# Three fused blocks on one core: low-rank inputs of the middle block inside its projection, and four junctions computed by halves of the tokens

## What is computed

```python
def second_block(x, ...):
    h = rmsnorm(x, pre_mix_g)
    proj = h @ w_in                                  # "win2"
    ya, yb, yc = split(proj)
    a_out = rwkv7_mixer(ya, ...)                     # token shift, low-rank decay, chunked recurrence
    b_out = moba_mixer(*split(yb, 3))                # attention
    c_out = gmlp_mixer(*split(yc, 2), ...)
    mix = concat(a_out, b_out, c_out) @ w_out        # "wout2"
    x = x + rmsnorm(mix, post_mix_g)
    h = rmsnorm(x, pre_ffn_g)
    gate, up = split(h @ w_ffn_in)                   # "ffin2"
    f = (silu(gate) * up) @ w_ffn_out                # "ffout2"
    return x + rmsnorm(f, post_ffn_g)

def rwkv7_mixer(ya, ...):
    prev = pad(ya)[:, :-1]
    ya = ya + mu * (prev - ya)                       # token shift
    r, k, v, wd, ad, gd = split(ya)
    w = -softplus(-(w0 + tanh(wd) @ w2)) - 0.5       # low-rank decay input
    a = sigmoid(a0 + ad @ a2)                        # low-rank input
    g = sigmoid(gd) @ g2
    kk = normalised(k * k_k)
    ...

def third_block(x, ...):
    h = rms_norm(x, norm_mix_pre)                    # then "win3a"
    x = x + rms_norm(hybrid_mixer(h, ...), norm_mix_post)      # ends in "wout3"
    f = square(relu(rms_norm(x, norm_mlp_pre) @ w_ff1)) @ w_ff2   # "ff1_3", "ff2_3"
    return x + rms_norm(f, norm_mlp_post)
```

## Time and profile before

| | |
|---|---|
| median of 3 runs | 3485.95 us |
| profiled execution | 3472.73 us, its span 3470.8 us |
| TensorE busy | 3293.9 us (95% of the span) |
| VectorE, ScalarE busy | 1159.3 us (33%), 553.4 us (16%) |
| chain that ended last | TensorE 84%, DMA 8%, VectorE 4%, ScalarE 3%, issue 1% |
| mean granted TensorE clock | 0.972 of full speed |

### The profile page before, as it was taken

How to read it: one execution, slowest core, us unless ns; L and a number is a source line. 1 busy time by engine, 2 the same in 40 slices (tenths; PEclk the granted TensorE clock), 3 DMA queues, 4 the chain that set the end, 5 groups by cost and what they waited for, 6 DMA issues and landing times.

```text
span 3470.8 us, 33312 instructions
## 1 busy us (share of the span) xinstructions
PE 3293.9 (95%) x13642; PEld 1788.8 (52%) x13642; DVE 1159.3 (33%) x2215; ACT 553.4 (16%) x1100; POOL 1.4 (0%) x6
## 2 busy tenths in 40 slices
PE   7999899999999999998799899999999999999998
PEld 4555444344333333376785378844444444378543
DVE  2046531111111111155653254401351893254101
ACT  2033220110011001213122310001232002200000
POOL 0000000000000000000000000000000000000000
PEclk9999999999999999999888999999999999999999
DMA  5122338999999999910000121212111221112210
GB/s 236 49 73 98 112 155 355 428 429 428 428 428 429 429 429 428 383 73 35 1 1 6 71 94 73 97 73 75 73 49 50 90 78 73 73 73 93 77 73 24
DMA packets 41082, 585.13 MB, mean 169 GB/s; under 512 B 4688, under 2 KB 4688, under 8 KB 5392
## 3 DMA queue, kind: packets, MB, share of 16 engines
q1 hardware_dynamic: 40752, 582.45, 41.2%
q0 software_dynamic: 224, 1.18, 0.1%
HBM read 581.51 MB, written 2.10 MB: 168 GB/s over the span
## 4 chain that ended last, share of the span: by engine, by line
PE 84%; DMA 8%; DVE 4%; ACT 3%; issue 1%; SPq 0%; DVEq 0%; ACTq 0%
PE PS L243 27%; PE PS L339 15%; PE PS L1139 10%; DMA ring<-in_weights 8%; PE PS L1119 4%; PE PS L547 3%; PE PS L279 3%; PE PS L730 3%; PE PS L1073 2%; PE PS L1936 2%; PE PS L1106 1%; PE PS L687 1%; PE PS L1055 1%; PE PS L553 1%; PE PS L1597 1%; PE PS L1924 1%
## 5 line engine op out<-in xcount | busy, mean ns | idle before, releaser
L243 PE MATMUL PS<-A,ring 128*128 128x512 f32 x1608 | 703.7, 600 | 15.1 <-DVEq L2215 7.2
L243 PEld LDWEIGHTS PS<-A,ring 128*128 128x128 f32 x1608 | 307.9, 192 | 407.3 <-issue 388.2
L1139 PE MATMUL PS<-A 128*64 128x512 f32 x1280 | 294.0, 601 | 2.3 <-DMA A<-in_weights 1.1
L339 PE MATMUL PS<-A 128*128 128x256 f32 x1056 | 235.1, 379 | 0.0
L243 PE MATMUL PS<-H,ring 128*128 128x512 f32 x544 | 234.3, 592 | 0.0
L339 PEld LDWEIGHTS PS<-A 128*128 128x128 f32 x1056 | 200.6, 190 | 27.3
L1119 PE MATMUL PS<-ring,A 128*64 128x512 f32 x768 | 173.2, 597 | 17.6 <-DMA ring<-in_weights 17.4
L1211 DVE TENSOR_TENSOR A<-A,PS 64x512 f32<-64x512 f32 x64 | 44.2, 690 | 420.9 <-ACT A L1168 420.9
L1139 PEld LDWEIGHTS PS<-A 128*64 128x64 f32 x1280 | 85.1, 137 | 176.9 <-issue 168.7
L1139 PE MATMUL PS<-ring,A 128*64 128x512 f32 x768 | 175.4, 598 | 0.8 <-DMA ring<-in_weights 0.3
L1514 DVE COPY H<-PS 128x512 f32<-128x512 f32 x32 | 22.1, 692 | 456.1 <-ACT A L1533 456.1
(11 more groups left out here) (448 smaller groups left out, 3511.7 us busy)
## 6 DMA issues: line engine op xcount, KB each, us to landing
ring<-in_weights SPq DMA_DIRECT2D x178, 2048.0 KB, 14.1
A<-in_weights SPq DMA_DIRECT2D x96, 2048.0 KB, 24.0
X<-in_x SPq DMA_DIRECT2D x1, 2048.0 KB, 10.8
out_y<-X SPq DMA_DIRECT2D x4, 512.0 KB, 2.6
con<-in_const SPq DMA_DIRECT2D x1, 1423.0 KB, 6.4
vec<-in_vec SPq DMA_DIRECT2D x1, 1075.0 KB, 15.0
A<-in_ctx SPq DMA_DIRECT2D x1, 1024.0 KB, 12.8
con<-in_levels POOLq DMA_DIRECT2D x1, 896.0 KB, 4.9
```

Of the source, the lines that this page charges most:

```text
L243: mm = nc.tensor.matmul(bank[:, 0:out_width], weight_tile(name, n), moving(k), start=k == 0, stop=k == k_tiles - 1)
L339: mm = nc.tensor.matmul(pair_bank(p, n), w[:, k, :], x[:, k, :], start=k == 0 and not more, stop=k == 3, skip_group_check=more)
L1139: mm = nc.tensor.matmul(PS[CAP * up:CAP * (up + 1), c % 2, :], XS[:, k, CAP * b:CAP * (b + 1)], w[:, n:n + 4, :].rearrange("p a b -> p (a ...
```

## The change

In the second block the token shifts begin with LO, GD and the keys, in pairs 4 to 9; `block1_out` runs twice a pair in pairs 0 to 3; k times k_k stands in pair 6. ScalarE takes tanh of LO and sigmoid of GD in pair 5. TensorE runs the six low-rank products in pair 6, after its second quarter product, in the four banks that the pair doesn't use, and ScalarE drains them there with sigmoids. After win2 VectorE does the running sums for p = 0 first, then the floors, p = 1, the normed MG, p = 2, two preparations, the gMLP gate, the third preparation. Tiles move in the arena so that nothing overlaps; the gate's banks are 6 and 7.

At the junctions the last output tile is computed for tokens 0 to 255 and then for 256 to 511, in two banks; ScalarE squares and copies each half, and mean, Ln, Exp, scaling, sum and `raw` are done by halves. The first half's mean stands on TensorE's queue after k = 3 of the second half, the second half's mean after k = 1 of the next projection's first half. `first_products` runs its four tiles over the first half and then over the second; the mean for the next norm comes after k = 2 of the second half. The number after `raw` is how many of the first half's tiles ScalarE makes before it turns to the second half's Ln and Exp (4, 8 and 4). At the end the output leaves in 2 transfers for the first half and 4 for the second.

```diff
+        def first_products_by_halves(pe, name, raw, sq):
+            base = S.next("pe", "raw", 16) - 16
+            banks = [open_bank(name, f) for f in range(4)]
+            for h in range(2):
+                for k in range(8):
+                    pe.wait_ge(S["raw"], base + 8 * h + k + 1)
+                    for f in range(4):
+                        mm = nc.tensor.matmul(banks[f][:, half_of(h)], weight_tile(name, 8 * f + k),
+                                              raw(k)[:, half_of(h)], start=k == 0, stop=k == 7)
...
+                    if h == 0 and k == 1:
+                        half_mean(pe, 1, sq)
+                    if h == 1 and k == 2:
+                        pe.wait_ge(S["sumsq"], S.next("pe", "sumsq"))
+                        nc.tensor.matmul(PS[:, 5, :], mean, H[:, 0, :], start=True, stop=True).then_inc(S["mean"], 1)
+        def half_mean(pe, h, sq):
+            if h == 0:
+                pe.wait_ge(S["msum"], S.next("pe", "msum"))
+            nc.tensor.matmul(PS[:, 5 + h, half_of(h)], mean, sq(0)[:, half_of(h)], start=True, stop=False)
+            pe.wait_ge(S["msq"], S.next("pe", "msq", 1 if h else 8))
+            nc.tensor.matmul(PS[:, 5 + h, half_of(h)], mean, sq(7)[:, half_of(h)], start=False, stop=True
+                             ).then_inc(S["mean"], 1)
+        def products_by_halves(pe, name, k_tiles, moving, sq):
+            products(name, range(7), k_tiles, moving)
+            for h in range(2):
+                for k in range(k_tiles):
+                    n = 7 * k_tiles + k
+                    mm = nc.tensor.matmul(PS[:, 4 + 3 * h, half_of(h)], weight_tile(name, n), moving(k)[:, half_of(h)],
+                                          start=k == 0, stop=k == k_tiles - 1)
...
+                    if h and k == 3:
+                        half_mean(pe, 0, sq)
+                mm.then_inc(S["last"], 1)
...
+        def last_half_act(act, h, sq):
+            act.wait_ge(S["last"], S.next("act", "last"))
+            bank = PS[:, 4 + 3 * h, half_of(h)]
+            nc.scalar.activation(sq(7)[:, half_of(h)], bank, ACT.Square).then_inc(S["msq"], 1)
+            nc.scalar.activation(H[:, 7, half_of(h)], bank, ACT.Copy)
...
+            if split < 8:
+                last_half_act(act, 1, sq)
+            pre_norm_half(act, 0, range(split), gain, raw)
+            nc.scalar.preload_act_table(ACT.Ln)
+            if split == 8:
+                last_half_act(act, 1, sq)
+            half_power_act(act, 1)
+            pre_norm_half(act, 0, range(split, 8), gain, raw)
+            pre_norm_half(act, 1, range(8), gain, raw)
             power_act(act)
...
-            post_norm_act(act, "wout2", RAW)
-            pre_norm_act(act, "pre_ffn", RAW)
+            post_norm_act(act, "wout2", RAW, "pre_ffn", RAW, 4)
...
             for p in range(10):
                 fast_out_dve(dve, "win2", p, a(4 + 2 * p), a(5 + 2 * p))
-                if p < 8:
-                    block1_out_dve(dve, p)
-                for j in (2 * p - 8, 2 * p - 7):
-                    if 0 <= j < 11:
-                        token_shift_dve(dve, j)
+                if p < 4:
+                    block1_out_dve(dve, 2 * p)
+                    block1_out_dve(dve, 2 * p + 1)
+                else:
+                    for n in (2 * p - 8, 2 * p - 7):
+                        if n < 11:
+                            token_shift_dve(dve, n)
...
-            for j in range(4):
-                sp.wait_ge(S["x_new"], 32 + 2 * j + 2)
-                sp.dma_start(out[:, 2 * j:2 * j + 2, :], X[:, 2 * j:2 * j + 2, :]).then_inc(S["stored"], 16)
+            for h, tiles in ((0, 4), (1, 2)):
+                for k in range(0, 8, tiles):
+                    sp.wait_ge(S["x_new"], 56 + 8 * h + k + tiles)
+                    sp.dma_start(out[:, k:k + tiles, TC * h:TC * h + TC], X[:, k:k + tiles, TC * h:TC * h + TC]
+                                 ).then_inc(S["stored"], 16)
```

More of the change, by code:

```diff
@@ L54 @@
     ("gate2", 0, 0, 3),
-    ("wout2", 8, 8, 8),
+    ("wout2", 8, 8, 7),
     ("ffin2", 2 * NFF2, 8, 4),
-    ("ffout2", 8, NFF2, 8),
+    ("ffout2", 8, NFF2, 7),
     ("win3a", 8, 8, 8),
@@ L343, in product @@
                     mm.then_inc(S["quarter"], 1)
+                if name == "win2" and p == LORA_PAIR + 1:
+                    all_drained(pe, "lora2", 6)
                 product(0, A11, HQ[0][0])
@@ L349, in fast_products @@
                 product(1, S2, T2)
+                if between:
+                    between(p)
                 if p == 0:
@@ L1851, in rwkv_tensor @@
         def rwkv_tensor(pe):
-            pe.wait_ge(S["lora_in"], 2)
-            for f in range(6):
-                bank = open_bank("lora2", f)
-                rows = slice(0, 64) if f < 3 else slice(64, 128)
-                nc.tensor.matmul(bank, vec[rows, VOFF["w2a2"][0] + f % 3 * P:VOFF["w2a2"][0] + (f % 3 + 1) * P],
-                                 A[rows, LO, :], start=True, stop=True).then_inc(S["product"], 1)
             for j in range(2):
```

195 lines of the change are left out of this document (116 added, 79 removed).

## The result

| | before | after |
|---|---|---|
| median (range, runs) | 3487.72 us (3485.44 to 3490.47, 4) | 3440.24 us (3439.24 to 3441.34, 4) |
| ratio after / before | | 0.9878 (95%: 0.9853 to 0.9902) |
| profiled execution | 3472.73, span 3470.8, clock 0.972 | 3439.27, span 3437.5, clock 0.978 |

The change is faster by 47.5 us by the medians, and by 33.5 by the two profiled executions. The forecast was 3461, with 3473 and 3453 as its ends: right in sign, wrong in size, and the median lies outside that range.

A forecast was written before the change was run, and what follows sets the result against it. TensorE, busy 95% of the span, bounds the kernel; only idle or slow stretches can be won. 8.2 + 4.1 + 3.3 + 8.1 + 4.5 = 28.2 us, less 3.4 for the clock, 24.8: 3485.95 - 24.8 = 3461 us, range 3453 to 3473.

The forecast's parts named there:

- the last one of the sum: Whole program: 24.8 us gained, taken off the runs' median 3485.95 rather than the profiled execution's 3472.73, giving 3461 us.
- Rival D: Recurrence behind the changed chain: short bursts hold the lower clock, 45 us longer, ending 20 us slower, 3506; chance 0.03.
- The second block: Win2's last quarter product to last preparation: 41.2 us for 54.6, 13.4 earlier; less 5.15 in pair 6, 8.2 gained.
- The low-rank term: Win2's pair 6: six low-rank calls, 12 records x 0.429 = 5.15 us longer, a cost.
- rival B: Second block gives nothing: TensorE waits in pairs 5 to 7 or the chain keeps its length; 16.6 gained, 3469; chance 0.12.
- ffout2's 8.1: Junction after ffout2: no gap left, 128 records and two means end at 2447.8 and not 2455.91, 8.1 us gained.
- wout2's 4.1: Junction after wout2: TensorE idle 2.7 us for 5.89, 4.1 us gained, before 1.7 us lost to the clock.
- rival A: Junctions after wout2 and wout3: the clock does not fall behind 2.7 us gaps; 28.2 us gained, 3458; chance 0.24.
- wout3's: Junction after wout3: same code as wout2's, 3.3 us gained, before 1.7 us lost to the clock behind a 2.7 us gap.
- Rival E: Junctions: halves run one behind the other, only the end and second block gain; 12.7 us, 3473; chance 0.06.
- Rival C: Junctions with 4 tiles ahead: a ScalarE table switch holds 1.38 us longer, TensorE starts 1.4 us later, 3464; chance 0.05.
- The end: Program's end: chain about 0.3 us shorter, 16 half-width VectorE instructions 6.0 us for 10.2, store stays 3.0; 4.5 us gained.

The follow-up runs named there:

- e1: The kernel before, unchanged, run again: median 3478.68 us, 6 executions short and 6 long.
- e4: The changed kernel, unchanged, run again: median 3441.29 us, 6 executions short and none long.
- e16: The changed kernel run again on another comparison's chip: median 3440.06 us, ratio to before 0.9889.
- e3: The changed kernel with its second block's part taken back, so only junctions and end go by halves: median 3464.17 us.
- e6: The kernel before with two useless calls on 64 rows in TensorE's idle time ahead of the last preparation's transposes: median 3473.09 us, 5 of 12 long.
- e7: The changed kernel with useless 128-row calls in TensorE's idle times at the junctions and ahead of wout2, ffout2, wout3 and ff2_3: median 3436.47 us.
- e9: The changed kernel with the MLP gate's four VectorE instructions back ahead of the three preparations: median 3460.64 us, 6 of 7 long.
- e10: The kernel before with only the gate's four VectorE instructions moved between the second and third preparation: median 3484.98 us, 9 of 12 long.
- e13: The changed kernel with the gate's four VectorE instructions moved on behind the start of the inverse: median 3454.05 us, 6 of 6 long.

## Why the prediction was wrong, point by point

**The step that failed** is the last one of the sum: "That execution is 13.2 us below the median of the runs, so for the median it is 3485.95 - 24.8". It took the 13.2 us as something that any kernel would carry along. They came from one stretch of before, the products within chunks, which by their lengths ran at the lower clock in 74 of 107 executions and then took 33.6 us for 17.5 (e1's profile and before's); none of the 16 executions of the change is long. Of the 20.9 us between 3461.15 (3485.95 - 24.8) and 3440.24, 13.2 are this offset, 8.7 is what the two profiled executions differ by beyond the 24.8 (4.3 at the attention's end, 2.6 before win2, the rest small), and 1.0 goes off again, because the change's profiled execution lies that far below its own median. So even against the profiled execution alone the 24.8 us were a quarter short of the 33.5 measured.

**Rival D had the mechanism and the wrong sign.** It said that the short bursts meet the clock at another time now, put the loss at 45 us, and ruled it out because "the runs of before, which meet it by chance too, lie within 5 us". The numbers at hand said otherwise: three runs at 3485 to 3490 and a profile at 3472.7 were two lengths, not a spread of 5. The stretch that differs is also another than the one D named (from 1800 us on): it lies at 1675 to 1708 us. The prediction's own last sign of being wrong, that "the stretch from the chunks within to wout2 has another length than before", holds against the long executions of before (16 us) and not between the two profiles (from the last transposes to wout2's start 253.1 us for 253.3).

**The second block.** From win2's last product to the last preparation 41.3 us for a forecast 41.2, the normed MG at +14.8 for +14.6: each step of that chain held within 0.3 us. The low-rank term was mis-sized: 3.81 us for 5.15, because records of 64 rows took 0.32 us where the sum had 0.429. The cover was there: no engine is late in pairs 5 to 7, so rival B falls. The earlier trace rows had a hint in them: 6.76 us for twelve records is little for records of 0.43 to 0.86, and before's clock stood at 0.50 for the first 6.0 of them.

**The junctions.** ffout2's 8.1 us held, and wout2's 4.1 measured 4.0, because the clock did not fall behind its 2.62 us gap (forecast 2.7), as rival A had it. Behind wout3's it did, and a second time behind the 3.04 us wait (forecast 3.2) further on: 3.4 us there, nothing at wout2, for 1.7 at each. The sum of the two was right, by luck. Rival E falls: the halves overlap. Rival C falls too, TensorE began when the forecast said.

**The end**: 5.0 us for 4.5; from the first scaling to the last sum 5.9 us for a forecast 6.0, the chain began 0.4 us earlier for 0.3, and the store behind the last sum, which the sum left at 3.0, took 2.7.

**Not foreseen**: 4.3 us at the attention's end, and 2.6 us before win2. The latter differ from one execution to the next and are no gain of the change: e4's trace of the same program is later by 2.7 us at win2's end and at its own end, e16's by 0.9 and 0.8.

## What to carry to other kernels

Where a profiled execution lies apart from the timed ones by more than these spread, ask first which stretch makes the difference, and profile the kernel again until both lengths are at hand; a constant offset is a guess that can be as large as the gain. Here the stretch was a long run of matmuls on 64 rows and 256 columns behind an idle time, and two calls of no use on all 128 rows, put into TensorE's idle time ahead of it, made all 12 executions short and cost nothing that can be told (median 3468.98 for 3468.9). Idle times of TensorE can cost more than their length, and whether they do varied from trace to trace with the same code: fill them when they can't be removed, but only where there is an idle time; the same calls at ffout2's junction, which has none, cost 2.14 us.

## What the runs showed of the hardware

- TensorE can be busy without its clock rising: the 24 pairs of products within chunks (64 rows, 256 columns a record) took 33.6 us in seven profiles (e1, e3, e6, e7, e9, e10, e13), in e1 busy 10.00 of 10 us at a granted clock of 0.50. Once at full clock the same records kept it (0.99 to 1.00 over 16 to 17 us). The Trainium skill (TensorE: Matmul & The Clock Gate, The HAM clock gate) has activity of TensorE release the throttle; the trace disagrees for these records, and agrees for the low-rank ones, also of 64 rows but 512 columns, under which the clock rose in five profiles of six.
- The clock can fall behind small idle times: after 1.36, 0.95, 0.69 and 0.69 us in a row it fell in nine profiles, and in eight it didn't, with the same code around them. Behind 2.62 us it fell after wout3 and not after wout2 in the change's profile.
- Twelve records of 64 rows and 512 columns took 3.81 us at full clock (0.32 each) where 128 rows take 0.43.
- A switch of ScalarE's table cost its 1.28 us: in the change's trace the Exp of the norm starts 0.02 us after the load's end (1629.72 + 1.28 to 1631.02). The page of the Trainium skill that the prediction names (ScalarE: Activation LUTs, What ACT_TABLE_LOAD costs) has 2.66.

```profile
1629.72 1.28 ACT L2118 ACT_TABLE_LOAD   x1
1631.02 1.95 ACT L2118 ACTIVATE A<-A,con 128x512 f32<-128x512 f32 x3
```
